# Grouped-key attention of a mixed block: values four steps behind scores instead of three, and VectorE rounds the probabilities in 8 of 44 steps

## The reference

```
def gqa_attend(q, k, v):
    s = jnp.einsum('bqhgd,bkhd->bhgqk', q, k).astype(jnp.float32) * (GQA_HEAD_DIM ** -0.5)
    p = jax.nn.softmax(s, axis=-1).astype(v.dtype)
    return jnp.einsum('bhgqk,bkhd->bqhgd', p, v)
```

## Time and profile before

| what | value |
|---|---|
| median of 3 runs | 3461.96 us (3459.22 to 3461.97) |
| profiled execution | 3465.23 us |
| its span | 3463.3 us |
| mean granted TensorE clock | 0.989 |
| busy share | PE 96%, DVE 65%, ACT 51%, POOL 44% |
| stage of the grouped-key steps | about 1785 to 2303 us of the span |
| one head of it | 32.05 us (2076.67 to 2108.72) |

### The profile page before, as it was taken

One profiled execution on the slowest core, in us unless ns is written; L12 is line 12 of the kernel. 1 busy time (PEld: TensorE's weight loads), 2 busy tenths in 40 slices (PEclk: granted clock), 3 DMA queues, 4 the chain that ended last, 5 costly groups with the idle time before them and its releaser, 6 DMA issues.

```text
span 3463.3 us, 47931 instructions
## 1 busy us (share of the span) xinstructions
PE 3330.5 (96%) x14993; PEld 2652.2 (77%) x14993; DVE 2261.4 (65%) x2647; ACT 1769.3 (51%) x3039; POOL 1538.4 (44%) x962
## 2 busy tenths in 40 slices
PE   7999999999999999999999999999998989999999
PEld 5778878778888888778777777778765668888877
DVE  6674878677576665638537777777558875555551
ACT  3343878332010101334339999971455558888880
POOL 3403444544444445410037777767220026666662
PEclk9999999999999999999999999999999999999999
DMA  2134232411213121123344434413255344232312
GB/s 103 49 115 136 55 86 52 154 53 55 85 47 99 49 85 58 61 70 118 117 116 99 96 82 95 106 49 109 100 198 157 124 120 129 58 81 67 70 36 80
DMA packets 196088, 313.56 MB, mean 91 GB/s; under 512 B 100928, under 2 KB 111680, under 8 KB 195968
## 3 DMA queue, kind: packets, MB, share of 16 engines
q1 hardware_dynamic: 195968, 312.01, 31.3%
HBM read 234.02 MB, written 77.92 MB: 90 GB/s over the span
## 4 chain that ended last, share of the span: by engine, by line
PE 66%; POOL 10%; issue 9%; DVE 9%; ACT 4%; DMA 1%; SPq 0%; POOLq 0%; DVEq 0%; ACTq 0%
PE PBX L283 11%; PE PBX L285 10%; PE PBX L284 10%; POOL gqa_pl L2366 8%; PE PMX L283 4%; PE PMX L284 4%; PE PMX L285 4%; PE PMX L2223 2%; PE PD L2268 2%; PE PD L2269 2%; PE PD L2270 2%; PE PBX L2250 2%; PE PBX L2249 2%; PE PBX L2251 2%; PE PD L1013 2%
## 5 line engine op out<-in xcount | busy, mean ns | idle before, releaser
L216 POOL TENSOR_TENSOR w_hi<-w_stage,zero 128x1024 fp32r<-128x1024 f32 (+2 forms) x116 | 223.6, 1927 | 1173.6 <-PE PBX L285 875.7
L2366 POOL TENSOR_TENSOR gqa_pl<-gqa_pf,gqa_ph 128x512 fp32r<-128x512 f32 (+1 forms) x288 | 381.6, 1342 | 146.8 <-ACT gqa_ph L2320 145.0
L2366 POOL TENSOR_TENSOR mla_pl<-mla_pf,mla_ph 128x512 fp32r<-128x512 f32 x256 | 341.9, 1341 | 207.8 <-ACT mla_ph L2320 202.3
L2388 DVE TENSOR_REDUCE mla_m<-PMX 128x1 f32<-128x1280 f32 x128 | 190.9, 1491 | 173.2 <-PE PMX L2223 173.0
L2388 DVE TENSOR_REDUCE gqa_m<-PMX 128x1 f32<-128x1280 f32 x144 | 201.6, 1400 | 150.5 <-PE PMX L2223 149.8
L218 POOL TENSOR_TENSOR w_lo<-w_stage,w_hi 128x1024 fp32r<-128x1024 f32 (+2 forms) x116 | 293.9, 2534 | 9.1
L1904 ACT ACTIVATE conv_in<-PBX 128x512 f32<-128x512 f32 x66 | 39.4, 599 | 478.9 <-PE PBX L285 474.9
L2314 ACT ACTIVATE mla_pf<-PBX 128x512 f32<-128x512 f32 x320 | 190.1, 594 | 82.1 <-PE PBX L2251 67.8
L2320 ACT ACTIVATE gqa_ph<-gqa_pf 128x512 fp32r<-128x512 f32 (+1 forms) x352 | 214.9, 611 | 12.4 <-PE PD L2270 0.4
L2314 ACT ACTIVATE gqa_pf<-PBX 128x512 f32<-128x512 f32 (+1 forms) x352 | 200.6, 570 | 31.0 <-PE PBX L2254 20.1
L283 PE MATMUL PBX<-ffn_hi,w_hi 128*128 128x512 f32 x528 | 207.2, 392 | 4.5 <-DVE ffn_lo L710 4.5
(11 more groups left out here) (526 smaller groups left out, 9961.5 us busy)
## 6 DMA issues: line engine op xcount, KB each, us to landing
mod_w<-in_w_mod SPq DMA_DIRECT2D x48, 512.0 KB, 3.5
w_stage<-in_w_up SPq DMA_DIRECT2D x44, 512.0 KB, 3.5
w_stage<-in_w_go SPq DMA_DIRECT2D x24, 512.0 KB, 3.7
gqa_k<-kh_d SPq DMA_DIRECT2D x32, 320.0 KB, 5.1
gqa_q<-qh_d SPq DMA_DIRECT2D x32, 320.0 KB, 6.8
w_stage<-in_w_down SPq DMA_DIRECT2D x24, 384.0 KB, 3.1
qh_d<-heads_qh SPq DMA_DIRECT2D x32, 256.0 KB, 2.0
ql_d<-heads_ql SPq DMA_DIRECT2D x32, 256.0 KB, 2.3
```

The costliest lines, as they stand in the source:

```text
L216: pool.tensor_tensor(w_hi[s][:, 0:st.cols], w_stage[s][:, 0:st.cols], z, ALU.add).then_inc(w_hi_done, 1)
L2366: eng.tensor_tensor(self.PL[k % 4][:, 0:n], self.PF[k % 4][:, 0:n], self.PH[k % 4][:, 0:n].bitcast(F32), ALU.subtract).then_inc(self.lo_dv ...
L2388: dve.tensor_reduce(self.M[g % 2][:, t:t + n], PMX[:, 0:n * w].rearrange("p (n w) -> p n w", n=n), AX.X, ALU.max, negate=True).then_inc(se ...
```

## The change

LAG becomes 4 for the grouped-key attention and stays 3 for the latent one. Values, `rden` and `final` all hang on LAG and move back by one step. In steps 7, 9, 13 and 19 of each head ACT no longer rounds: `low` on DVE first makes PH (a `tensor_copy`), waits for it, and subtracts. The semaphore `hi` counts only the steps of ACT, `hi_dve` those of DVE.

```diff
--- before.py
+++ after.py
@@ -2016,7 +2016,6 @@
 
 
 
-            LAG = 3
 
             def __init__(self, name, scope, chunks, keys, scale, layout, mix, first, first_maxima):
                 self.name, self.chunks, self.keys, self.scale, self.mix = name, chunks, keys, scale, mix
@@ -2031,6 +2030,8 @@
                 self.D = [first_maxima[0], scope.sb(f"{name}_d1", [P, 4, P], R32)]
                 self.M = first_maxima[1]
                 self.dim = 96 if self.mla else 64
+
+                self.LAG = 3 if self.mla else 4
                 self.nq = chunks[-1][0] + chunks[-1][1]
                 self.load_inc = 16 * (4 if self.mla else 6)
 
@@ -2071,6 +2072,7 @@
                 self.fin_all = HEADS * self.NC + CR_FIN2
                 self.norm_all = HEADS * self.NC + CR_N
 
+                self.hi_dve = None if self.mla else sem(f"{name}_hi_dve")
                 self.dve_lo = lambda k: k % (self.SB // 2) in ((3, 8, 13, 18) if self.mla else (7, 9, 13, 19))
                 self.lags = (self.LAG + 4, self.LAG + 4, 0) if self.mla else (self.LAG + 5, self.LAG + 2, self.LAG + 3)
                 self.n_dve = sum(1 for k in range(self.SB) if self.dve_lo(k))
@@ -2125,6 +2127,15 @@
                 n = self.n_dve if mine else self.n_pool
                 eng.wait_ge(self.lo_dve if mine else self.lo_pool, i * n + (b * n + count))
 
+
+            def dve_hi(self, k):
+
+                return not self.mla and self.dve_lo(k)
+
+            def upto(self, k):
+
+                mine = self.dve_lo(k)
+                return sum(1 for x in range(k + 1) if self.dve_lo(x) == mine), self.n_dve if mine else self.n_pool
 
             def load_k(self, sp, q, kv_row):
                 K = self.K[q]
@@ -2314,7 +2325,8 @@
                     act.activation(self.PF[k % 4][:, 0:n], self.S[k % 2][:, 0:n], ACT.Exp, scale=self.scale)\
                        .then_inc(self.exp, 1)
                     between()
-
+                    if self.dve_hi(k):
+                        return
                     act.wait_ge(self.pv, i * SB + (k - 4 + CR_PV2 + 1))
                     act.wait_ge(self.exp, i * SB + (k + CR_E + 1))
                     act.activation(self.PH[k % 4][:, 0:n], self.PF[k % 4][:, 0:n], ACT.Copy).then_inc(self.hi, 1)
@@ -2362,7 +2374,16 @@
 
             def low(self, eng, i, k):
                 n = self.chunks[self.steps[k][1]][1]
-                eng.wait_ge(self.hi, i * self.SB + (k + 1))
+                count, per_pair = self.upto(k)
+                if self.dve_hi(k):
+                    eng.wait_ge(self.exp, i * self.SB + (k + CR_E + 1))
+                    eng.wait_ge(self.pv, i * self.SB + (k - 4 + CR_PV2 + 1))
+                    eng.tensor_copy(self.PH[k % 4][:, 0:n], self.PF[k % 4][:, 0:n]).then_inc(self.hi_dve, 1)
+                    eng.wait_ge(self.hi_dve, i * per_pair + count)
+                elif self.mla:
+                    eng.wait_ge(self.hi, i * self.SB + (k + 1))
+                else:
+                    eng.wait_ge(self.hi, i * per_pair + count)
                 eng.tensor_tensor(self.PL[k % 4][:, 0:n], self.PF[k % 4][:, 0:n], self.PH[k % 4][:, 0:n].bitcast(F32),
                                   ALU.subtract).then_inc(self.lo_dve if self.dve_lo(k) else self.lo_pool, 1)
```

## The result

| | before | changed |
|---|---|---|
| median of 5 runs, us | 3460.56 (3459.22 to 3461.97) | 3480.18 (3471.71 to 3481.11) |
| ratio, 95% interval | | 1.0044 (1.0033 to 1.0055) |
| span of the profiled execution, us | 3463.3 | 3479.2 |
| mean granted TensorE clock | 0.989 | 0.988 |
| one head of the stage, us | 32.05 | 33.15 (2083.05 to 2116.20) |

What follows compares the result with a forecast made beforehand. PE paces the stage, waiting for POOL's low halves. Later broadcasts +19.5, stalls behind them -4.5, those at head ends -7.5, first head some -0.5: +7 us, 3472 profiled, 3469 median; range 3450 to 3481, the forecast's own 3464 to 3475.

Steps and rivals of the forecast that it cites:

- a longer chain: VectorE's run of `rden` and `final` work frees the broadcast's bank at 13.3 us: +19 us, 3481; chance 0.17 with a second wait.
- POOL's waits go: PE's stalls for POOL's low halves, before step 8, before step 10 and after step 20, vanish: 1.9 us a head.
- `rden` and `final` make a chain on VectorE that holds PE twice: Late `rden` delays `final` on DVE; PE waits at step 6's maxima and step 8's broadcast, 2.4 us.
- the 1.3 us by which the broadcast moves: Broadcast of step 8 comes at 12.5 us instead of 11.2 in 15 heads: +19.5 us.
- the second rival: Longer chain (+19 us, 3481), or added roundings stretch beside POOL: 0.5 us at two places, +16 on the forecast; chance 0.17.
- the gains behind the broadcast: After step 8's broadcast, stalls of 0.3 us and, at the head's end, 0.5 us go in 15 heads: -4.5 and -7.5.
- ScalarE's relief is worth nothing: ACT loses 4 roundings a head in steps 7 to 19; no gain, since PE sets the pace; otherwise 2.2 us.
- its rounding behind the values costs nothing: ACT's rounding waits for values right behind the scores: 0.07 us where ACT isn't behind, nothing on PE's path.
- The wait for the exponential of step 3: Scores 5 wait for ACT, which ends at 6.6 with PE there at 6.3; inside the larger wait, adding nothing.
- The room behind the reductions of steps 10 and 14: On DVE, 1.4 us before the next maxima holds a rounding of 0.43 and a low half of 0.7.
- The durations beside POOL: On DVE, gate product 1.22 and diagonal 1.51 us were taken, not 0.85 and 1.21, because POOL is busy.

Runs made afterwards that it cites:

- first run: The changed kernel with `rden` and `final` back in the steps where they stood before, only the values a step later: 3448.41 us, ratio 0.9965 against the kernel before.

## Why the prediction was right, and where its size was off

**The number.** I gave 3469 us and the median was 3480.18: the direction was right and the size too small. The time lies outside the forecast's own 3464 to 3475, at the very edge of the wide range (3450 to 3481), and so in the band of +13 us and more that I gave to a longer chain, with a chance of 0.17. That it is still inside the wide range owes something to luck.

**POOL's waits go.** Right: 43.2 us became 0.6. Their worth, 1.9 us a head, was too high: with both obstacles away a head took 30.6 us, 1.4 less than before, where the unstalled sum was 30.2. In that version PE still waited 0.3 to 0.45 us before the maxima of step 6 for the reduction of step 4, which I had taken to hold nothing.

**`rden` and `final` make a chain on VectorE that holds PE twice.** Right, and shown part by part: undoing both turns +15 into -12 us, moving only `rden` gives -10, only the `final` of chunk 2 +3. The distances within the chain were as worked out but for the gate product; the table counts from the head's first scores.

| | worked out | measured |
|---|---|---|
| scores of step 2 | 2.92 | 3.23 |
| exponential of step 2 | 3.66 | 3.99 |
| first product of the chain | 5.6 | 5.99 |
| reduction of step 4 | 7.6 | 8.22 |
| small reduction | 10.5 | 11.14 |
| broadcast of step 8 | 12.5 | 13.04 |

**The term that was too small is the 1.3 us by which the broadcast moves: it was 1.8 in a head at full clock.** Two things made it so. First, I had written that the added roundings stand "behind `final`, not in front of anything that PE needs in steps 0 to 8": the rounding of step 19 took 1.51 us, not 0.43, and its low half 1.11; the reduction of step 0 then ended at 2085.54, and the maxima of step 2 waited. That is 0.3 us a head, and with ScalarE rounding step 19 the head fell by just that. Second, the gate product in the chain took 1.47 us, not 1.22: 0.25 us. Together 0.55 x 15 = 8 us. In the first the second rival was right: it said that a rounding made while POOL works stretches.

**The clock.** I had no term for it. Four of the 14 heads of the profiled execution took 0.85 us longer (33.92 against 33.07), together 3.4 us. The windows of one microsecond behind the wait of 1.81 us in such a head (columns: window; PE, PEld, DVE, ACT, POOL busy; granted clock; DMA share; GB/s):

```profile
1858.00:1859.00 1.00, 0.28 (x2) 0.00 (x0) 0.97 (x2) 1.00 (x2) 1.00 (x1) 1.00 0.99 206
1859.00:1860.00 1.00, 0.34 (x2) 0.34 (x3) 0.86 (x2) 0.94 (x4) 1.00 (x2) 0.96 1.21 167
1860.00:1861.00 1.00, 1.00 (x5) 0.81 (x4) 1.00 (x2) 0.47 (x1) 0.91 (x2) 0.50 1.34 217
...
1863.00:1864.00 1.00, 1.00 (x5) 0.82 (x4) 0.42 (x1) 0.74 (x2) 0.79 (x1) 0.83 0.00 0
```

The granted clock falls to 0.50, the lower level of 1.2 GHz, for some 3 us. In part the loss hides behind the wait before the broadcast: in these four heads PE has none there.

**The sum.** The 14 heads between the first and the last, by the starts of PE's instructions, mean of each part in us:

| part of a head | before | changed | moved | forecast |
|---|---|---|---|---|
| to the broadcast of step 8 | 11.20 | 13.32 | +2.12 | +1.3 |
| from there to the scores of step 10 | 3.44 | 3.21 | -0.23 | -0.3 |
| to the scores of step 20 | 14.35 | 14.34 | 0 | 0 |
| to the next head | 3.03 | 2.44 | -0.59 | -0.5 |
| whole head | 32.02 | 33.32 | +1.30 | +0.5 |

So the gains behind the broadcast came about as forecast, and the whole miss is in the first row: about 8 us through the chain's size and 3 through the clock. The 14 heads are +18.1 us, the first one -0.55 (forecast: -0.5), the last +0.8 up to its last values: from the stage's first scores to its last values +18.4, against +7. The span shows only +15.9, because the changed kernel's profiled execution reached the stage 3.4 us sooner (first scores at 1781.28 instead of 1784.63), in code that both kernels share, and lost 0.9 behind it. The difference of single executions is thus uncertain by some us.

**ScalarE's relief is worth nothing, and its rounding behind the values costs nothing.** Right: with POOL still the limit the relief gave 1.0005, and with the ends early the version in which ScalarE makes every rounding right behind the values is one of the two fastest. The wait for the exponential of step 3 was there (0.50 us at 2090.11) and lay inside the next one.

**The room behind the reductions of steps 10 and 14.** In the changed kernel it held: the rounding of step 7 took 0.41 us (2097.05, below), and PE doesn't wait at step 12. With the ends early it took 1.52 and the room was gone: 0.87 us at step 12. The rival that named this was right on the mechanism, but not for this place of the changed kernel.

**The durations beside POOL.** I took the long ones of the earlier trace rows because POOL would be busy. That reason doesn't separate them from the short ones of the earlier trace rows: POOL was busy then too. In the kernel before, the gate product of 0.85 us at 2104.03 lies inside this run in GpSimd's timeline:

```profile
2100.07 7.22 POOL L2366 TENSOR_TENSOR gqa_pl<-gqa_pf,gqa_ph 128x512 fp32r<-128x512 f32 x5 [2.32 <-ACT gqa_ph L2320]
```

That the long durations, and longer ones, came was therefore not shown by my argument. Not tried: whether the start of the gate product against that of POOL's instruction decides; the runs show many values (0.70 to 1.58 us in 28 of the changed kernel's products, POOL at work throughout each) but don't vary this alone.

## What to carry to other kernels

A lag that one constant sets for several followers moves all of them. Before it is raised, see which of them free a buffer that a leading engine waits for, here the product that empties the bank of the broadcast, and keep these where they were. Then look at the engine that carries them: work that hides today behind a stall comes to the front when the stall goes.

## What the runs showed of the hardware

In the changed kernel's stage a rounding of 128x512 on VectorE took 0.41 to 0.43 us in all 41 cases in which POOL was idle, and 1.40 to 1.62 in 16 of the 17 in which POOL worked throughout (0.81 in one). In the changed kernel POOL's run from 2075.48 covers the one at 2081.48 (above), and this one, in VectorE's timeline, lies between two of its runs:

```profile
2097.05 0.41 DVE L2381 CAST gqa_ph<-gqa_pf 128x512 fp32r<-128x512 f32 x1
```

The runs in GpSimd's timeline (start, duration over all of a run):

```profile
2075.48 9.25 POOL L2387 TENSOR_TENSOR gqa_pl<-gqa_pf,gqa_ph 128x512 fp32r<-128x512 f32 x7 [2.68 <-ACT gqa_ph L2332]
...
2089.52 7.32 POOL L2387 TENSOR_TENSOR gqa_pl<-gqa_pf,gqa_ph 128x512 fp32r<-128x512 f32 x5 [1.78 <-ACT gqa_ph L2332]
2098.58 1.28 POOL L2387 TENSOR_TENSOR gqa_pl<-gqa_pf,gqa_ph 128x512 fp32r<-128x512 f32 x1 [1.74 <-ACT gqa_ph L2332]
```

POOL at work isn't enough for the long duration. With the ends early (first run) seven roundings took 0.40 us although POOL worked throughout; one of them, in VectorE's timeline, and POOL's run around it:

```profile
2066.44 0.40 DVE L2381 CAST gqa_ph<-gqa_pf 128x512 fp32r<-128x512 f32 x1
...
2059.99 9.87 POOL L2387 TENSOR_TENSOR gqa_pl<-gqa_pf,gqa_ph 128x512 fp32r<-128x512 f32 x7 [1.77 <-ACT gqa_ph L2332]
```

What decides is open. The Trainium skill (GPSIMD Engine Reference, the table with the row on SBUF interfaces) names contention with VectorE instructions in a two-port mode as well as with two SBUF inputs. The rounding has one input; the trace doesn't show in which mode it ran, and agrees with the row only in that most roundings beside POOL were long. I had applied the row to the products of the chain and priced the rounding at 0.43 us, from the earlier trace rows, a stage in which POOL was idle at every one of them; beside POOL it was mostly 1.4 or 1.5.

The wait of PE's weight loads before the maxima of step 6 was 1.81 us in seven of the 15 heads of the changed kernel that follow another and 1.68 or 1.69 in eight, by turns. The granted clock fell to 0.50 behind four of the seven, every fourth head, and behind none of the eight. With the second wait removed (`final` of chunk 2 early) the first stayed, at up to 1.8 us, and no head was longer than 32.41 us. What decides is open. The runs of the changed kernel differ in the clock too: the one of 3471.71 us had a mean granted clock of 0.993, that of 3481.11, the profiled one, 0.988. Whether this place makes the difference isn't shown: runs of the kernel before spread likewise, from 3454.54 us at 0.994 to 3469.05 at 0.988.
